# A front with products first, half units in GpSimd's queue, and feed-forward input weights that move

## The reference, cut to what matters

```
h = _rmsnorm(x, norm_ffn_g[l])
gate, up = jnp.split(jnp.einsum('bsd,df->bsf', h, w_ffn_in[l]), 2, axis=-1)
x = x + jnp.einsum('bsf,fd->bsd', jax.nn.silu(gate) * up, w_ffn_out[l])
```

## Time and profile before

| | |
|---|---|
| median of 3 runs | 3067.46 us (3066.72 to 3068.49) |
| profiled execution, its own time | 3068.92 us |
| its span in the profile | 3067.1 us |
| mean granted TensorE clock, of full speed | 0.951 |
| TensorE busy | 2788.3 us (91%), 16468 matmuls |
| VectorE busy | 1891.5 us (62%), 2400 instructions |
| ScalarE busy | 1299.4 us (42%) |
| GpSimd busy | 24.4 us (1%) |
| moved by transfers | 644.59 MB, mean 210 GB/s |

### The profile page before, as it was taken

One profiled execution on the slowest core, in us unless ns is written; L12 is line 12 of the kernel. 1 busy time (PEld: TensorE's weight loads), 2 busy tenths in 40 slices (PEclk: granted clock), 3 DMA queues, 4 the chain that ended last, 5 costly groups with the idle time before them and its releaser, 6 DMA issues.

```text
span 3067.1 us, 42249 instructions
## 1 busy us (share of the span) xinstructions
PE 2788.3 (91%) x16468; PEld 2409.3 (79%) x16468; DVE 1891.5 (62%) x2400; ACT 1299.4 (42%) x1609; POOL 24.4 (1%) x46
## 2 busy tenths in 40 slices
PE   2669999897899999999799898999889999999998
PEld 0248888676788787778599386999779998998996
DVE  5996765456666788988766544454554455445454
ACT  1024443343344567777433043534344543443443
POOL 0000000000000000000000000000000000000000
PEclk9779998798899999999899997999999999999999
DMA  8588666331577799999445252544444455545553
GB/s 319 227 324 287 246 251 217 123 110 46 192 255 251 264 321 363 370 368 373 191 151 178 82 185 87 187 176 172 149 175 164 177 193 183 186 179 192 187 182 124
DMA packets 144715, 644.59 MB, mean 210 GB/s; under 512 B 10923, under 2 KB 10988, under 8 KB 89048
## 3 DMA queue, kind: packets, MB, share of 16 engines
q1 hardware_dynamic: 136416, 593.53, 53.5%
q0 software_dynamic: 5344, 30.93, 2.8%
q10 hardware_dynamic: 2840, 18.56, 1.7%
HBM read 635.59 MB, written 7.39 MB: 210 GB/s over the span
## 4 chain that ended last, share of the span: by engine, by line
PE 71%; DVE 14%; DMA 8%; ACT 4%; issue 3%; DVEq 0%; ACTq 0%; SPq 0%
PE ps L1497 70%; DMA raw<-in_stream 5%; DVE raw L952 3%; DVE w_lo L869 3%; ACT w_hi L550 2%; DMA under_r<-in_stream 1%; DVE under_r L964 1%; DMA arena<-in_dft_k 1%; DVE h_lo L920 0%; DVE arena L928 0%; ACT arena L665 0%; DVE arena L1024 0%; ACT arena L571 0%; DVE arena L1037 0%; DVE arena L1417 0%
## 5 line engine op out<-in xcount | busy, mean ns | idle before, releaser
L869 DVE TENSOR_TENSOR w_lo<-raw,w_hi 128x1024 fp32r<-128x1024 f32 x968 | 1169.8, 1223 | 768.1 <-ACT w_hi L550 765.5
L550 ACT ACTIVATE w_hi<-raw 128x1024 fp32r<-128x1024 f32 x968 | 1009.4, 1056 | 779.0 <-PE ps L1497 685.4
L1497 PE MATMUL ps<-h_hi,w_hi 128*128 128x256 f32 x2944 | 843.0, 286 | 23.8 <-DVE h_lo L920 17.0
L1497 PE MATMUL ps<-h_lo,w_hi 128*128 128x256 f32 x2944 | 839.3, 285 | 0.0
L1497 PE MATMUL ps<-h_hi,w_lo 128*128 128x256 f32 x2944 | 839.0, 285 | 0.0
L1497 PEld LDWEIGHTS ps<-h_hi,w_hi 128*128 128x128 f32 x2944 | 571.9, 194 | 25.9 <-issue 24.4
L1497 PEld LDWEIGHTS ps<-h_lo,w_hi 128*128 128x128 f32 x2944 | 571.7, 194 | 0.2
L1497 PEld LDWEIGHTS ps<-h_hi,w_lo 128*128 128x128 f32 x2944 | 571.5, 194 | 0.0
L1497 PE MATMUL ps<-w_hi,r_hi 128*128 128x512 f32 x1184 | 470.2, 397 | 11.1 <-DVE w_lo L869 4.4
L1497 PE MATMUL ps<-w_lo,r_hi 128*128 128x512 f32 x1184 | 463.1, 391 | 0.0
L1497 PE MATMUL ps<-w_hi,r_lo 128*128 128x512 f32 x1184 | 462.8, 391 | 0.0
(11 more groups left out here) (266 smaller groups left out, 1925.0 us busy)
## 6 DMA issues: line engine op xcount, KB each, us to landing
raw<-in_stream SPq DMA_DIRECT2D x524, 1024.0 KB, 5.0
under_r<-in_stream SPq DMA_DIRECT2D x80, 512.0 KB, 5.7
arena<-in_mod_units ACTq DMA_DIRECT2D x16, 1024.0 KB, 4.8
filters<-arena POOLq DMA_DIRECT2D x4, 1280.0 KB, 5.7
arena<-filters POOLq DMA_DIRECT2D x4, 1280.0 KB, 6.1
x<-in_x POOLq DMA_DIRECT2D x1, 2048.0 KB, 18.9
arena<-bias_rows POOLq DMA_DIRECT2D x2, 1024.0 KB, 6.9
x<-bias_rows POOLq DMA_DIRECT2D x2, 1024.0 KB, 10.4
```

The lines of the kernel that those rows point to most:

```text
L550: act.activation(dst, src, ACT.Copy).then_inc(hi_ready, 1)
L869: dve.tensor_tensor(low, src, high, ALU.subtract).then_inc(lo_ready, 1)
L1497: return pe.matmul(o, a, b, start=start, stop=stop)
```

## The change

**Front.** VectorE makes the first two modulation products before it looks at the bias rows and the small network, and one more product in the third layer's place (2, 2, 3). `dft_k` gets a semaphore of its own, which TensorE waits for only before the Fourier matmuls. `make_taps` is cut in two pairs, with one product between them and the others behind them. The first two `lo` pieces of the weights come after twelve tiles of `h1` instead of eight.

**Asides.** The halves leave SyncE's queue and are issued by GpSimd, in runs between the tables; `ASIDE` has three in four steps instead of two in three, zeros at four steps near the Toeplitz tables, and two instead of five at `GAP_AT`. `ld_cmp` goes ahead of the Toeplitz table 1.

**Normalizations.** `h2`, `hs` and `hf` turn into other PSUM banks, and the first product after each waits for the pieces of `h_lo` that it reads, not for all four. For `hs` the first two halves of the experts' weights are rounded and split between the tiles.

**Feed-forward.** The input products become token-major, with the stored units gathered as in the expert stage: eleven blocks of eight units, each with one silu of 1024 columns, one product, eight transposes and a split. These phases and `out2` are written out without loops.

```diff
+TOEPLITZ_AT = (7, 8, 13, 14)
...
-            counts.append(1 if k % 3 < 2 else 0)
+            counts.append(0 if k % 4 == 3 or k in TOEPLITZ_AT else 1)
...
+TURN_BANKS = {"h2": (4, 5, 6, 7), "hs": (2, 3, 6, 7), "hf": (4, 5, 6, 7)}
...
+    return any(0 <= n - BASE[f"ffn_in{part}"] < SIZE[f"ffn_in{part}"] for part in range(3))
...
-            aside(0)
-            aside(1)
-            weight(4)
-            used = 0
-            for k in range(len(ASIDE)):
-                if k % 2 == 0:
-                    weight(k // 2 + 5)
-                for _ in range(ASIDE[k]):
-                    aside(used + 2)
-                    used += 1
-            for n in range(len(ASIDE) // 2 + 5, BASE["moe"]):
+            for n in range(SLOTS, BASE["moe"]):
                 weight(n)
             sp.wait_ge(sem("routed"), 1)
...
-            stream(group_base("hyena"), UNITS // SLOTS)
+            stream(group_base("hyena"), group_base("ffn_in0"))
+            for part in range(3):
+                for n in range(SIZE[f"ffn_in{part}"]):
+                    unit = BASE[f"ffn_in{part}"] + n
+                    first = ADA_UNITS + unit - n % 8
+                    quarter = sp_units[first:first + 8].rearrange("(j w) p n -> w p j n", w=2)[n // 4 % 2][:, :, n % 4 * 512:n % 4 * 512 + 512]
+                    sp.wait_ge(lo_ready, 2 * unit - 6)
+                    sp.dma_start(raw[:, n % SLOTS, :].rearrange("p (j n) -> p j n", j=4), quarter).then_inc(landed[n % SLOTS], 16)
+                stream(group_base(f"ffn_down{part}"), group_base(f"ffn_down{part}") + SIZE[f"ffn_down{part}"] // SLOTS)
...
+            def aside(first, last):
+                for j in range(first, min(last, ASIDE_HALVES)):
+                    if j >= 2:
+                        pool.wait_ge(sem("aside_done"), j - 1)
+                    pool.dma_start(aside_slot[:, j % 2, :], d["stream"][FIRST_UNITS + j // 2][:, j % 2 * HALF:(j % 2 + 1) * HALF])\
+                        .then_inc(sem(f"aside_landed{j % 2}"), 16)
+            def issued(k):
+                return sum(ASIDE[:k]) + 2
+            aside(0, issued(0))
...
+            load("ld_sink", (stat[:, 32:40], d["sinks"].partition_broadcast(P)))
+            aside(issued(0), issued(7))
             toeplitz(0, toep)
+            aside(issued(7), issued(13))
             toeplitz(2, toep2)
-            load("ld_sink", (stat[:, 32:40], d["sinks"].partition_broadcast(P)))
+            aside(issued(13), issued(56))
             pool.wait_ge(sem("att_out"), 16 * 2)
+            load("ld_cmp", (w1k, d["w1k"]), (w1v, d["w1v"]), (w2c, d["w2kv"]), (peT, d["pe"]))
+            aside(issued(56), issued(62))
             toeplitz(1, toep2)
-            load("ld_cmp", (w1k, d["w1k"]), (w1v, d["w1v"]), (w2c, d["w2kv"]), (peT, d["pe"]))
+            aside(issued(62), issued(74))
             pool.wait_ge(sem("cmp_hidden"), 2)
             toeplitz(3, toep)
+            aside(issued(74), ASIDE_HALVES)
             pool.wait_ge(sem("att_out"), 16 * 3)
             load("ld_x", (x[:, 1, :], x_rows[:, 1, :]))
             pool.wait_ge(sem("att_out"), 82)
...
+            act.dma_start(at(F_DFT, 1280), d["dft_k"]).then_inc(sem("ld_dft"), 16)
...
-            for k in range(3):
-                hi(gm, k)
+            def moe_hi():
+                hi(gm, 0)
+                hi(gm, 1)
+            norm_hi("hs", h_hi, DC, hf, 0, moe_hi)
+            hi(gm, 2)
...
+            def ffn_hi(q, b):
+                act.wait_ge(sem("ffn_t"), q + 1)
+                for h in range(TH):
+                    ins = copy(r_hi[:, 4 * b:4 * b + 4, h * P:(h + 1) * P], ps[:, 6 + h, :].rearrange("p (f n) -> p f n", f=4))
+                ins.then_inc(sem("ffn_hi"), 1)
...
+                def ffn_step(g, i, k, q0=q0):
+                    if k == 2 and i:
+                        ffn_hi(q0 + i - 1, i - 1)
+                    if k == 7:
                         done(g, k)
-                        act.wait_ge(sem("ffn_pair"), 2 * i + (n0 + f + 1))
-                        act.activation(g_act[:, f, :], ps[:, k // 2, 0:T], ACT.Silu).then_inc(sem("ffn_silu"), 1)
-                    elif k % 4 == 3:
-                        act.wait_ge(sem("ffn_pair"), 2 * i + (n0 + f + 3))
-                        copy(r_hi[:, bass.ds(2 * i + f, 1), :], hid[:, f:f + 1, :]).then_inc(sem("ffn_hi"), 1)
-                phase(f"ffn_in{part}", ffn_step)
-                phase(f"ffn_down{part}")
+                        if q0 + i:
+                            act.wait_ge(sem("ffn_pair"), q0 + i)
+                        act.activation(g_tok[:, :, :], ps[:, 0:2, :], ACT.Silu).then_inc(sem("ffn_silu"), 1)
...
+                        if split and c >= 7:
+                            low(c - 7)
+                        if early and c == early_at:
                             early()
...
+            modulation(0, 2)
...
-                modulation(2 * n, 2)
-            modulation(6, 6)
+                modulation(2 * n + 2, 3 if n == 2 else 2)
...
+            dve.wait_ge(sem("ld_block"), 48)
+            make_taps(0, 0, 2)
+            modulation(9, 1)
+            make_taps(0, 2, 4)
+            modulation(10, 2)
...
-                    make_taps(b + 1)
-                modulation(done_units, 7)
+                    make_taps(b + 1, 0, 2)
+                modulation(done_units, 1)
+                if b < 3:
+                    make_taps(b + 1, 2, 4)
...
+            norm_split("h1", (h_hi, h_lo), DC, hf, 0, gain, mod[:, 0:DC], early=first_lo, early_at=11)
...
+            def ffn_lo(q, b):
+                dve.wait_ge(sem("ffn_hi"), q + 1)
+                for h in range(TH):
+                    o = slice(h * P, (h + 1) * P)
+                    ins = dve.tensor_tensor(r_lo[:, 4 * b:4 * b + 4, o], ps[:, 6 + h, :].rearrange("p (f n) -> p f n", f=4),
+                                            r_hi[:, 4 * b:4 * b + 4, o].bitcast(F32), ALU.subtract)
+                ins.then_inc(sem("ffn_lo"), 1)
...
+                def ffn_step(g, i, k, q0=q0):
+                    if k == 3 and i:
+                        ffn_lo(q0 + i - 1, i - 1)
+                    if k == 15:
                         done(g, k)
-                        dve.wait_ge(sem("ffn_silu"), 2 * i + (n0 + f + 1))
-                        dve.tensor_tensor(hid[:, f, :], g_act[:, f, :], ps[:, k // 2, 0:T], ALU.mult).then_inc(sem("ffn_pair"), 1)
-                        dve.wait_ge(sem("ffn_hi"), 2 * i + (n0 + f + 1))
-                        dve.tensor_tensor(r_lo[:, bass.ds(2 * i + f, 1), :], hid[:, f:f + 1, :],
-                                          r_hi[:, bass.ds(2 * i + f, 1), :].bitcast(F32), ALU.subtract).then_inc(sem("ffn_lo"), 1)
-                phase(f"ffn_in{part}", ffn_step)
-                per_cb = FFN_TILES[part] // 4
-                phase(f"ffn_down{part}", add_cols(8 + 4 * part, per_cb), per_iter=2 if per_cb == 4 else 3)
+                        dve.wait_ge(sem("ffn_silu"), q0 + i + 1)
+                        if q0 + i:
+                            dve.wait_ge(sem("ffn_t"), q0 + i)
...
-            pe.wait_ge(sem("ld_filt"), 80)
+            pe.wait_ge(sem("ld_filt"), 64)
...
+            pe.wait_ge(sem("ld_dft"), 16)
...
+                        if k == 2:
+                            turn_hidden(hidden + per_cb - 1)
+                        if cb == 0 and k % 2 == 0:
+                            pe.wait_ge(sem("ffn_lo"), hidden + kq + 1)
...
+                    if p == 0 and k < 8 and k % 2 == 0:
+                        pe.wait_ge(sem("norm_lo"), norm_count("hs", "lo", k // 2 + 1))
...
+            def hyena_step(g, i, k):
+                pe.wait_ge(sem("norm_lo"), norm_count("h2", "lo", 4 if k else 2))
+                if k % 2 == 0:
+                    pe.wait_ge(sem("conv_out"), 4 * i + (k // 2 + 1))
+                return feature_major(k, ps[:, k // 2, 0:T])
+            phase("hyena", hyena_step)
...
+            def turn_hidden(q):
+                pe.wait_ge(sem("ffn_pair"), q + 1)
+                if q:
+                    pe.wait_ge(sem("ffn_lo"), q)
+                if q in (4, 8):
+                    pe.wait_ge(sem("cols_added"), 2 + 8 + q)
+                for h in range(TH):
+                    for f in range(4):
+                        ins = pe.transpose(ps[:, 6 + h, f * P:(f + 1) * P], hid_tok[:, h, f * P:(f + 1) * P], ident)
+                ins.then_inc(sem("ffn_t"), 1)
...
+                def gate_up(g, i, k, q0=q0):
+                    u = k // 2
+                    if q0 + i == 0 and k < 8 and k % 2 == 0:
+                        pe.wait_ge(sem("norm_lo"), norm_count("hf", "lo", k // 2 + 1))
+                    if k == 0 and q0 + i:
+                        pe.wait_ge(sem("ffn_silu"), q0 + i)
+                    if k == 8 and q0 + i:
+                        pe.wait_ge(sem("ffn_pair"), q0 + i)
+                    if k == 2 and i:
+                        turn_hidden(q0 + i - 1)
+                    return token_major(k, u % 4, 4, 2 * (u // 4), H)
```

(37 more changed lines are left out.)

88 lines of the change are left out of this document (35 added, 53 removed).

## The result

The changed kernel took 3038.85 us (median of 4 runs, 3037.57 to 3050.54), the kernel before 3067.97 beside it: ratio 0.991, 95% interval 0.9891 to 0.9928. Run again on another chip it took 3035.25 us beside 3074.09: 0.9876, 0.9859 to 0.9892. So the gain is 29 and 39 us. The forecast was 48.6 us and 3019, with a range of 3006 to 3033: the sign was right, the size too large, and both medians lie above the range.

A forecast was written before the change was run, and what follows sets the result against it. It took TensorE to bound the feed-forward part, VectorE's late start and holes the front, and an engine chain attention. Terms 20.6 - 0.5 + 0.5 + 4.0 + 24.0 = 48.6 us off the 3067.46 median gave 3019, range 3006 to 3033.

The forecast's parts named there:

- reciprocal near 60: Sign in the front: the reciprocal after the first taps, at 75.02 before, would start near 60 us.
- `a_q` near 192: Sign at the front's end: TensorE's a_q would come near 192 us.
- the line on `under_r`: Sign against the forecast: wrong if VectorE's waits for under_r in attention exceed 10 us.
- Half units: Refills moved to GpSimd's queue: a loss of 0.5 us, ends a gain of 3 and a loss of 12.
- rival "slower": GpSimd's refills land late, by port or ring, in the 24 attention steps: 3086 at 8.5 us landings; chance 0.03.
- Front: Stretch before a_q: earlier modulation products and filled waits between taps gain 14.8 + 5.8 = 20.6 us.
- the second term: Front, four filter blocks: products put into the waits between taps gain 5.8 us.
- The first term: Front up to the first reciprocal: start moves from 75.0 to 60.2, a gain of 14.8 us, set by transfers.
- the first rival: Front held by transfers: only some 5 of the 14.8 us come, 3029 us; chance 0.14.
- `hs`: Start after the hs normalization: the stall moves three halves on, a gain of 0.5 us.
- `h2`: Start after the h2 normalization: first half unit needs two h_lo pieces instead of four, a gain of 4.0 us.
- Feed-forward: Feed-forward part: 28.0 from wider matmuls, less 9.7 for turns and 1.1, plus 6.8 from hf start: 24.0 us gained.

The follow-up runs named there:

- e4: Changed kernel, half units still issued by GpSimd, but with the old table of counts: 3035.06 us, ratio 0.9875.
- e2: Changed kernel with half units back in SyncE's queue, the old table of counts and the old order of GpSimd's tables: 3029.04 us, ratio 0.9851.
- e1: The changed kernel run again with no edit, for a profile of a typical execution: 3035.25 us, ratio 0.9876.
- the first profile: Profiled execution of the changed kernel's first four runs, no edit, the slowest of them: 3050.54 us.
- e7: e2 with only half the columns of each of the first forty modulation units loaded, the rest set to zero: 3013.61 us, ratio 0.9805.
- e12: e2 with two front tables issued later and the experts' fourth and fifth w_lo made before VectorE's register loads: 3013.09 us, ratio 0.981.

## Why the prediction was wrong, point by point

The first two lines of "what would show it" came true (first product at 11.2, feed-forward part 729.5 us with one idle of 1.04), "reciprocal near 60" and "`a_q` near 192" did not (64.7, and 195.5 for the second half of `a_q`, from whose 212.4 the 192 was counted), and the line on `under_r` was the one that told: 65.8 us of waits.

- **Half units: the step that failed.** "In the projection stretches TensorE has three half units in hand and shows no idle", so that only 24 attention steps could lose 0.3 us each, -0.5 in all. Measured: +6.0 us for the queue (e4 against e2) and +6.2 for queue and table (e1 against e2) by the medians; +10.3 for both in e1's attention part, 18.4 in the first profile. The attention steps lost little or nothing: the three of them take 168.6 us before, 171.8 in e2, 167.1 in e1 and 171.8 in the first profile. The loss lies in the projections, which I had called covered: `a_q` to `a_v` takes 70.1 us in e1 against 65.2 in e2, `c_k` and `c_v` 63.5 against 55.5. The cover was there but thin: VectorE's work and waits filled 59 of 66.7 us before, 68.0 of 68.7 after. I took TensorE's idle of zero as a margin; it only says that the margin wasn't yet used up. And I priced the queue alone. The table of counts, which I described but did not cost, brings 17 of the refills back after two steps instead of three. A step is 2.9 us at TensorE's pace (24 matmuls of 0.120 us), and outside the attention steps a refill takes 5.9 us from product to landing at the median in e1 and 8 us or more in a fifth of the cases. The rival "slower" named late landings, but in the wrong place and at the wrong size.
- **Front: mechanism right, size off.** 14.8 + 5.8 = 20.6, measured 15.4 at the mark of `a_q` and 17.4 at the third `w_lo`, which lies behind the same work in both. The waits between taps are gone, and the second term held: from the reciprocal to the third `w_lo` 6.3 us less in e1. The first term came to 10.3 to 11.0: I had divided 11.0 MB by 385 GB/s, a rate worked out from a share of 0.82; at shares of 0.94 to 1.02 the core moved 346 to 371. And it moves more than the sum's 20.2 MB by then: 355 GB/s over 64.72 us are 23.0 MB, since units behind the twelfth are asked for too. e7 shows that transfers hold it, which was the sum's own assumption and the first rival's; the truth lies between the two.
- **`hs`: wrong sign.** 0.5 gained by the forecast, about 2 lost in the runs. The stall was foreseen, its place and cause too; what was missing is the lower clock behind it, and e12 turns it to some 4 us gained.
- **`h2`: right.** 4.0 forecast. TensorE's start stands 7.04 us after its last work before and 2.90 after:

```profile
1549.31 0.57 PE L1546 MATMUL ps<-h_hi,w_hi 128*128 128x256 f32 x1 [2.90 <-DVE h_lo L950]
```

- **Feed-forward: right, 2 us too small.** 24.0 forecast, 26.1 measured. The chain after (start, length, what): 192 matmuls of 512 columns in 43.55 us (0.2268 each), then a turn, 44.43 in all, so 0.88 a turn; and the one stall.

```profile
2304.91 49.21 PE ps L1546 x216
2355.00 43.55 PE ps L1546 x192
2399.43 43.55 PE ps L1546 x192
...
2979.86 54.66 PE ps L1546 x240
```

```profile
2979.86 0.47 PE L1546 MATMUL ps<-w_hi,r_hi 128*128 128x512 f32 x1 [1.04 <-DVE r_lo L1516]
```

The 2 us are the clock again, this time in favour. Before, TensorE stood 7.25 us and then had 0.50 and, on the mean, 0.52 over its first 4.66 us, by an estimate 2.2 us lost; after, it comes out of its turns with 0.26 us idle and keeps the full clock. First before, then after:

```profile
2304.34:2308.00 3.66, 3.66 (x17) 3.66 (x18) 1.22 (x1) 0.71 (x1) 0.00 (x0) 0.50 0.15 22
```

```profile
2304.91:3034.40 729.49, 728.45 (x3256) 603.69 (x3256) 364.97 (x327) 300.69 (x297) 0.00 (x0) 1.00 0.55 183
```

The rates of 120.0 and 226.8 ns held, not the formula of the Trainium skill (TensorE: Matmul & The Clock Gate, Back-to-back issue gap). The prediction left out that the section gives the formula for an isolated matmul; for a stream with weight loads it has about 131 ns for 512 columns, which no run here shows either.

Put together, by the third `w_lo`: -3.2 front, -11.8 half units (-5.2 and -9.8 by the table's marks), -2.0 `hs`, +0.8 `h2`, +2.1 feed-forward: 14.1 of the 48.6 us missing, and 34.5 is what e1's profile has. These are stages of one profile; by the medians the half units cost 6.2 us.

## What to carry to other kernels

A stage without idle on its bounding engine has no known margin: add up work and waits of the engine that feeds it, and cost a change of its waits against what is left. For a pair of slots that are refilled, the number to compare with the time from product to landing is the shortest distance between two uses of one slot, not their mean rate; bunching cost as much here (5.7 us) as the slower queue (6.0). A long stall of TensorE was paid twice here: after 2.90 us (`h2`), 3.43, 4.14 and 7.25 us it went on at a granted clock of 0.50, 0.57, 0.50 and 0.50 for some 3 to 5 us, after 1.04 us and less it kept 1.00. So move the work that ends the stall first, and only then the start.

## What the runs showed of the hardware that was not expected

GpSimd's issue of a 512 KB refill holds it 0.53 us, in each of 24 cases within 0.02, where SyncE's takes 0.33. Transfers at a share of 0.94 to 1.02 moved 346 to 371 GB/s in the front, where a share of 0.82 had suggested 385. The same kernel took 3067.97 us on one chip and 3072.7 to 3074.8 on others, while the changed one went the other way, from 3038.85 to 3035.25, though its first four runs lie 13 us apart.
